# Nine waits moved or shortened in a one-core kernel: mixer, feed-forward changes, latent attention

## The reference, cut to what matters

```python
for i in range(2):
    h = h + 0.5 * swiglu(rmsnorm(h, ln_ffn1[i]), w1_gate[i], w1_up[i], w1_down[i])   # 1024 -> 2816 -> 1024
    u = rmsnorm(h, ln_mix[i])
    h = h + (mamba2_mixer(u, ...) if i == 0 else latent_attention(u, ...))
    h = h + 0.5 * swiglu(rmsnorm(h, ln_ffn2[i]), w2_gate[i], w2_up[i], w2_down[i])
    h = h + (p[i] @ w_ple_in[i]) * sigmoid(rmsnorm(h, ln_ple[i]) @ w_ple_gate[i])
    if i == 0: latent keys = rmsnorm(rmsnorm(h, ln_kv) @ w_kv_a)      # shared by all streams
```

## Time and profile before

| | |
|---|---|
| median of 3 runs | 1906.42 us (1904.54 to 1907.23) |
| the profiled execution's own time | 1900.23 us |
| its span in the profile | 1898.4 us |
| PE busy in the span | 1832.8 us, 97% |
| DVE, ACT, POOL busy | 1140.4, 825.7, 249.8 us |
| the chain that ended last | PE 83%, DVE 9%, ACT 4% |

### The profile page before, as it was taken

The page is one execution under the profiler, slowest core; times in us unless marked ns, Lnnn a source line. Parts: engine busy times, 40 slices in busy tenths (PEclk is TensorE's granted clock), DMA queues, the critical chain, the costliest instruction groups (busy, mean ns, idle before and its releaser), DMA issues.

```text
span 1898.4 us, 28238 instructions
## 1 busy us (share of the span) xinstructions
PE 1832.8 (97%) x10552; PEld 1742.0 (92%) x10552; DVE 1140.4 (60%) x1703; ACT 825.7 (43%) x1425; POOL 249.8 (13%) x298
## 2 busy tenths in 40 slices
PE   9999999999999999999999999988998999999997
PEld 8999998798887899999999999985777889999997
DVE  6554447878888655444765544455777746455444
ACT  5333325665464433333553333345665534333233
POOL 1000110422221000011400001222112130000110
PEclk9999999999999999999999999999999999999999
DMA  6444444456352544444344444441124533444441
GB/s 204 128 119 129 134 143 145 151 189 227 117 200 84 176 127 120 129 145 133 112 142 122 121 132 142 136 140 37 45 82 128 170 118 113 133 125 121 142 136 64
DMA packets 67652, 249.71 MB, mean 132 GB/s; under 512 B 8328, under 2 KB 9608, under 8 KB 66288
## 3 DMA queue, kind: packets, MB, share of 16 engines
q1 hardware_dynamic: 57584, 205.32, 35.9%
q0 software_dynamic: 9984, 43.24, 6.8%
HBM read 235.74 MB, written 12.12 MB: 131 GB/s over the span
## 4 chain that ended last, share of the span: by engine, by line
PE 83%; DVE 9%; ACT 4%; issue 2%; DMA 1%; POOL 0%; SPq 0%; DVEq 0%; ACTq 0%; POOLq 0%
PE pair L1805 23%; PE pair L1806 23%; PE pair L1807 23%; PE pair L2300 1%; PE pair L2218 1%; DVE wlo L1195 1%; PE pair L2219 1%; PE pair L2220 1%; DVE cy L1321 1%; PE pair L1812 1%; PE pair L1814 1%; PE pair L1813 1%; ACT seg L835 1%; PE pair L2002 1%; DVE S L1417 1%
## 5 line engine op out<-in xcount | busy, mean ns | idle before, releaser
L1805 PE MATMUL pair<-xh,whi 128*128 128x384 f32 x1928 | 652.9, 339 | 16.2 <-DVE xl L1205 13.4
L1806 PE MATMUL pair<-xl,whi 128*128 128x384 f32 x1928 | 647.1, 336 | 0.0
L1807 PE MATMUL pair<-xh,wlo 128*128 128x384 f32 x1928 | 646.9, 336 | 0.0
L1195 DVE TENSOR_TENSOR wlo<-raw,whi 128x1024 fp32r<-128x1024 f32 (+3 forms) x372 | 464.7, 1251 | 185.4 <-ACT whi L706 176.1
L706 ACT ACTIVATE whi<-raw 128x1024 fp32r<-128x1024 f32 (+2 forms) x369 | 378.7, 1029 | 290.8 <-PE pair L1807 276.7
L1805 PEld LDWEIGHTS pair<-xh,whi 128*128 128x128 f32 x1928 | 364.1, 189 | 26.3 <-issue 14.9
L1806 PEld LDWEIGHTS pair<-xl,whi 128*128 128x128 f32 x1928 | 364.3, 189 | 1.6 <-issue 1.0
L1807 PEld LDWEIGHTS pair<-xh,wlo 128*128 128x128 f32 x1928 | 364.1, 189 | 0.0
L1215 DVE TENSOR_TENSOR tg<-pair,rstd 128x384 f32<-128x384 f32 x88 | 49.0, 557 | 331.2 <-PE pair L1807 330.5
L1805 PE MATMUL pair<-ah,whi 128*128 128x384 f32 x704 | 237.0, 337 | 3.5 <-DVE tu L1216 3.3
L1807 PE MATMUL pair<-ah,wlo 128*128 128x384 f32 x704 | 236.6, 336 | 0.0
(11 more groups left out here) (394 smaller groups left out, 2285.1 us busy)
## 6 DMA issues: line engine op xcount, KB each, us to landing
raw<-in_stream SPq DMA_DIRECT2D x372, 512.0 KB, 3.6
S<-in_ssm POOLq DMA_DIRECT2D x4, 2048.0 KB, 9.2
out_ssm_s<-S POOLq DMA_DIRECT2D x4, 2048.0 KB, 8.1
seg<-acs_rows POOLq DMA_DIRECT2D x12, 512.0 KB, 6.1
cTb<-in_cacheT POOLq DMA_DIRECT2D x10, 512.0 KB, 4.0
kn<-rs_rows SPq DMA_DIRECT2D x16, 264.0 KB
lowC<-in_cache SPq DMA_DIRECT2D x8, 512.0 KB, 3.2
lowA<-in_cacheT POOLq DMA_DIRECT2D x6, 512.0 KB, 5.2
```

The source lines that it names most:

```text
L1195: V.tensor_tensor(wlo[:, r, 0:w], raw[:, r, 0:w], whi[:, r, 0:w].bitcast(F32), ALU.subtract).then_inc(lo_ready, 1)
L1805: M(out, whi[:, r, ws], mh_(k), start=first and k == k0, stop=False)
L1806: M(out, whi[:, r, ws], ml_(k), start=False, stop=False)
L1807: ins = M(out, wlo[:, r, ws], mh_(k), start=False, stop=last and k == k1 - 1)
```

## The change

It touches nine places. The arithmetic is the same but for two forms (the last of the y squares is added by PE; the compressed queries are scaled once, straight from PSUM). In the listing "..." marks what is left out.

1. **Mixer's order.** In table and engine programs: `in 0, in 1, in 2, out 0, in 3, out 1, in 4` in place of `in 0, in 1, out 0, in 2, out 1, in 3, in 4`.
2. **State products.** Four in a call, in four banks; two calls in a group. The first call stands between y tiles 1 and 2, the second behind `in 1` of the next group (last group: behind the first output block).
3. **Mixer's end.** Three y squares are summed on POOL, the fourth by a second matmul. POOL does `last_part`. `residual(2)` and `(3)` follow each other, weight splits move behind what PE waits for, the state adds move behind the norm's sums.
4. **Feed-forward.** `down` waits for the first last pair only, and for the second before its third product.
5. **Behind KV.** The splits of h go ahead of the token norm; PE waits for `kvr` before its third block.
6. **Compressed queries.** The 512-wide copies are gone; each token tile is finished on its own in the last block.
7. **First prompt scores** go ahead of half of the values; key weights, values and past splits are interleaved.
8. **First units.** The first maximum goes ahead of the last two absorbed parts, the second key split behind the first unit; Exp is loaded three parts earlier.
9. **Sample heads.** Two head pairs per bank in four banks; the first output block starts by the tile; the last two output blocks run side by side, so that the splits of h begin seven tiles before the end.

```diff
-order += [("in", g, 0), ("in", g, 1), ("out", g - 1, 0), ("in", g, 2), ("out", g - 1, 1), ("in", g, 3), ("in", g, 4)]
+order += [("in", g, 0), ("in", g, 1), ("in", g, 2), ("out", g - 1, 0), ("in", g, 3), ("out", g - 1, 1), ("in", g, 4)]
...
+            return bank[(6, 7, 4, 5, 4, 7, 5, 6)[i] if g == GROUPS - 1 else (6, 7, 4, 5, 4, 5, 0, 3)[i]]
...
 (POOL, last group)
+                    pool.wait_ge(y_rstd, 1)
+                    pool.wait_ge(f_evac, 8 * g)
+                    pool.tensor_tensor(facc[:, 6:8, :], facc[:, 6:8, :], bc(rstd[:, 0, :], (P, 2, TOK), 1),
+                                       ALU.mult).then_inc(h_part, 1)
+                    pool.wait_ge(h_part, 1)
+                    pool.tensor_tensor(h[:, 6:8, :], h[:, 6:8, :], facc[:, 6:8, :], ALU.add).then_inc(h_part, 1)
...
 (DVE, group g)
                     in_proj(g, 1)
+                    state_add(g - 1, 2)
                     state_add(g - 1, 3)
-                    out_proj(g - 1, 0)
                 in_proj(g, 2)
+                    out_proj(g - 1, 0)
...
 (DVE, mixer's end)
-            last_part()
-            for b in range(4):
+            for b in range(2):
                 residual(b)
+                lo_split(n + 4 + b)
                 x_lo(2, 2 * b)
                 x_lo(2, 2 * b + 1)
-                if b < 3:
-                    lo_split(n + 4 + b)
+            residual(2)
+            residual(3)
+            for k in range(4, KD):
+                x_lo(2, k)
+            lo_split(n + 6)
...
 (DVE, compressed queries)
-            for t in range(TT):
-                V.tensor_scalar(cqr[:, t, :], bank[t][:, :], rows[:, 1, t:t + 1], None, ALU.mult).then_inc(cq_ready, 1)
             dve.wait_ge(w_ld, 16 * 5)
             for t in range(TT):
                 dve.wait_ge(cq_std, t + 1)
                 step(V.reciprocal(rsc[:, t, 4:5], rsc[:, t, 2:3]))
+                step(V.tensor_tensor(rsc[:, t, 4:5], rsc[:, t, 4:5], rows[:, 1, t:t + 1], ALU.mult))
...
 (PE)
             def down(u, m):
-                pe.wait_ge(gu_evac, 2 + KF * (u + 1))
+                pe.wait_ge(gu_evac, 1 + KF * (u + 1))
                 for j in range(KD):
+                    if j == 2:
+                        pe.wait_ge(gu_evac, 2 + KF * (u + 1))
...
+                for j in range(4):
                     rows32 = slice(32 * j, 32 * j + 32)
+                    ins = M(state_bank(g, 4 * e + j)[:, :], Bm[rows32, e, :], xw[rows32, 2, :], start=True, stop=True)
...
-            M(bank[5][:, 0:TOK], ones[:, :], sqacc[:, 0, :], start=True, stop=True).then_inc(y_sum_ps, 1)
+            M(bank[5][:, 0:TOK], ones[:, :], sqacc[:, 0, :], start=True, stop=False)
+            pe.wait_ge(y_sq, 4 * GROUPS)
+            M(bank[5][:, 0:TOK], ones[:, :], zs[:, 3, :], start=False, stop=True).then_inc(y_sum_ps, 1)
...
+            pe.wait_ge(q_kept, 12)
+            p_values(0)
+            p_values(1)
+            pe.wait_ge(key_kept, 4)
+            pe.wait_ge(key_rows_ready, ITEMS)
             p_scores(0)
             p_scores(1)
+            p_values(2)
+            p_values(3)
+            pe.wait_ge(wk_lo, 2)
...
+            for k in range(KD):
+                for b in (6, 7):
+                    ins = product(bank[2 + b % 4][:, 0:TOK], (WO + b) % SLOTS, k, k + 1, *X, k == 0, k == KD - 1)
+                    if b == 6 and k == KD - 1:
+                        ins.then_inc(blk, 1)
+                if k < KD - 1:
+                    ins.then_inc(wo_ps, 1)
```

More of the change, by code:

```diff
@@ L935, in _ @@
             kx_hi(KD - 1)
-            for b in range(3):
-                hi_split(KV + b + 3)
+            hi_split(KV + 3)
+            hi_split(KV + 4)
+            act.wait_ge(blk, CRED + PG + KD)
+            for k in range(KD - 2):
+                x_hi(4, k)
+            hi_split(KV + 5)
+            for k in range(KD - 2, KD):
+                x_hi(4, k)
             def token_std(m, x):
@@ L1124, in _ @@
                 ins.then_inc(qc_hi, 1)
+                if j == 5:
+                    act.preload_act_table(ACT.Exp)
                 if j == 3:
@@ L1206, in x_lo, with gate_up @@
                                        in1=xh[:, k, :].bitcast(F32), op0=ALU.mult, op1=ALU.subtract).then_inc(xl_ready, 1)
-            def gate_up(u, m, norm_sums=None):
+            def gate_up(u, m, norm_sums=None, behind=None):
                 base, r = BASE[f"gu{u}"], rstd[:, m % 2, :]
@@ L1224, in pair @@
                         V.tensor_tensor(al[:, f, :], tu[:, j, :], ah[:, f, :].bitcast(F32), ALU.subtract).then_inc(al_ready, 1)
-                lo_split(base + 3)
                 if norm_sums is not None:
                     norm_sums()
+                lo_split(base + 3)
+                if behind is not None:
+                    behind()
                 if m != 4:
@@ L1444, in out_proj @@
                 f_add(g, b)
-            def last_part():
-                step(V.tensor_tensor(facc[:, 6:8, :], facc[:, 6:8, :], bc(rstd[:, 0, :], (P, 2, TOK), 1), ALU.mult))
-                V.tensor_tensor(h[:, 6:8, :], h[:, 6:8, :], facc[:, 6:8, :], ALU.add).then_inc(h_part, 1)
             def residual(b):
@@ L1513, in _ @@
                 y_rows(g)
-                if not last:
-                    state_add(g, 2)
             n = out_block(GROUPS - 1, 0)
@@ L1550, in _ @@
             kx_lo(KD - 1)
-            for b in range(3):
-                lo_split(KV + b + 3)
+            lo_split(KV + 3)
+            lo_split(KV + 4)
+            for k in range(KD - 2):
+                x_lo(4, k)
+            lo_split(KV + 5)
+            for k in range(KD - 2, KD):
+                x_lo(4, k)
             def token_rows(x):
@@ L1748, in _, with absorbed @@
             keys_split(0)
-            for j in range(8):
+            def absorbed(j):
                 dve.wait_ge(qc_hi, j + 1)
@@ L1755, in _ @@
                 ins.then_inc(qc_ev, 1)
+            for j in range(6):
+                absorbed(j)
             def s_max(u):
@@ L1769, in _ @@
             s_max(0)
-            keys_split(1)
+            absorbed(6)
+            absorbed(7)
             for u in range(UNITS):
@@ L1789, in _ @@
                 V.tensor_tensor(h[:, b, :], h[:, b, :], bank[2 + b % 4][:, 0:TOK], ALU.add).then_inc(h_new, 1)
-            for k in range(KD):
+            lo_split(WO + 9)
+            for k in range(6):
                 x_lo(6, k)
+            for b in (6, 7):
+                dve.wait_ge(blk, CRED + WO + b + 1)
+                V.tensor_tensor(h[:, b, :], h[:, b, :], bank[2 + b % 4][:, 0:TOK], ALU.add).then_inc(h_new, 1)
+            x_lo(6, 6)
+            x_lo(6, 7)
+            lo_split(WO + 10)
             gate_up(3, 6)
@@ L1830, in pair @@
                         pe.wait_ge(gu_evac, i * 2 + (KF * u + j + 1))
+                        if first and j and m == 4:
+                            pe.wait_ge(kvr_ready, TT)
                         for half in range(2):
@@ L2343, in _ @@
                     pe.wait_ge(h_new, 48 + b - 3)
-                product(bank[2 + b % 4][:, 0:TOK], (WO + b) % SLOTS, 0, KD, *X, True, True).then_inc(blk, 1)
+                for k in range(KD):
+                    if b == 0 and k % 2 == 0:
+                        pe.wait_ge(ol_ready, MH // 2 + k // 2 + 1)
+                    ins = product(bank[2 + b % 4][:, 0:TOK], (WO + b) % SLOTS, k, k + 1, *X, k == 0, k == KD - 1)
+                ins.then_inc(blk, 1)
+            weights(WO + 6)
+            weights(WO + 7)
+            pe.wait_ge(h_new, 48 + 4)
+            for k in range(KD):
+                for b in (6, 7):
+                    ins = product(bank[2 + b % 4][:, 0:TOK], (WO + b) % SLOTS, k, k + 1, *X, k == 0, k == KD - 1)
+                    if b == 6 and k == KD - 1:
+                        ins.then_inc(blk, 1)
+                if k < KD - 1:
+                    ins.then_inc(wo_ps, 1)
+            ins.then_inc(blk, 1)
             gate_up(3, 6)
```

205 lines of the change are left out of this document (102 added, 103 removed).

## The result

The changed kernel takes 1872.08 us (median of 4 runs, 1871.61 to 1874.61), the kernel before 1905.48 in the same comparison. The ratio is 0.9829, with a 95% interval of 0.9814 to 0.9843: 32.6 us less (30 to 35). Forecast were 1878.0 in a range of 1869 to 1889, and 28.5 us of gain. The profiled execution takes 1872.35 us, 27.9 less than the profiled one before. The medians lie 33.4 apart, since the profiled execution before, at 1900.23, was a short one of its kernel.

The account below looks back on a forecast made before the run. PE, busy 97% of the span, was taken as the bound. Gains 3.0 + 7.0 + 4.2 + 2.2 + 0.5 + 4.9 + 1.0 + 5.7 = 28.5 us off the 1906.4 median gave 1878 us, range 1869 to 1889.

Parts of the forecast that it names:

- A: Mixer's groups: four-product calls and new block order gain 3.0 us despite new waits for S; bounds −0.5 to 5.
- E: Compressed queries: gain 0.5 us, mostly hidden behind the transfer of wv; bounds 0 and 4.8.
- D: Behind KV: gate_up(2) no longer waits for xl, less 0.7 of new wait; gain 2.2 us, bounds 0 to 3.
- F: First prompt scores: waits vanish, second expansion of past keys begins at 1317.1; gain 4.9 us, bounds 2 to 6.
- G: First units: second unit's scores wait less for Pb, unit 2 comes 0.5 to 1.1 earlier; gain 1.0 us.
- B: Mixer's end: shorter DVE chain to the last xl, POOL helping, half clock shrinking; gain 7.0 us, bounds 2.5 to 10.
- the first rival: Mixer's groups and units: clock falls in the new waits, each fall costing 1.5 us; total 1883; chance 0.15.
- The third rival: Mixer's end: POOL blocks DVE, costing 5.6 in place of 1.5 us; total 1882; chance 0.08.
- C: Start of down: waits for tu vanish at three of four, 1.4 us each; gain 4.2 us, bounds 3.3 to 4.5.
- H: Heads and output: heads take 3.8 us, block begins 2.7 earlier, gate_up(3) waits go; gain 5.7 us, bounds 3 to 6.5.
- The second: State products: four not side by side, a call takes 2.3 us; some 3 us lost, total 1881; chance 0.11.
- The slower one: New waits for S, at the units and behind KV leave half-clock stretches that eat the gain; ≥ 1910; chance 0.02.

Follow-up runs that it names:

- x_pool_late: Changed kernel, with POOL summing the y squares of groups 0 to 2 only behind the second output block; 1867.77 us, ratio 0.9809.
- x_both: Changed kernel, with POOL's y square sum later and DVE's third pair of state adds before the second input block; 1863.53 us, ratio 0.9779.
- x_a_undone: Changed kernel, with output blocks back in place and state products two in a call for groups 0 to 2; 1871.61 us, ratio 0.9829.
- x_last_dve: Changed kernel, with scaling and adding of the last two tiles of h at the mixer's end moved from POOL to DVE; 1868.87 us, ratio 0.9810.
- x_w_split: Changed kernel, with the three small loads counted apart from wk and wv ahead of the compressed queries; 1871.03 us, ratio 0.9819.
- x_s_early: Changed kernel, with DVE adding the third pair of states before the second input block; 1874.61 us, ratio 0.9851.
- x_again: The changed kernel once more, without an edit; 1873.19 us, ratio 0.9835.

## Why the prediction was right, and which steps failed

**The total** was right, 1878 against 1872.1, in a range of 1869 to 1889. The sum was 28.5 us and the profiled executions lie 27.9 apart, but in this two errors meet: A with the stretch ahead of it is 7.4 short, E, D, F and G are 6 over and B is 1 over. That they cancel is luck. By medians the gain is 33.4. At most some 8 of the 27.9 us came through the clock, an estimate from the mean granted clock of the two executions: 0.990 over 1898 us and 0.994 over 1871 us leave 19 and 11 us of full clock not granted. The sum named such a gain in B (2.5) and in D alone.

**A. Products of the groups**, 3.0 forecast, −0.9 measured in their stretch. Step by step: the call was taken as 1.45 between bounds of 1.2 and 2.3 and is 1.07, below the lower bound, since 1.2 had been read up to the second matmul behind the call (364.98), past a restart. Nothing but the restart is paid for the second pair. The new wait for `S` was worked out as 2.2 and is 1.97, 2.25, 2.24. The step that failed is "the wait of 0.44 for `facc` also goes, as DVE is ahead by then". DVE was not ahead: the first output block's add now comes behind input block 2, into POOL's squares, and the wait grew to 0.98 and 1.60. x_pool_late and x_both show this. With some 1.6 us of half clock at the third place, in its stead, that is 4.2 us, about the distance from 3.0 to −0.9. The price of such a meeting stood in the earlier trace rows, and I used it for B alone. Also, one of the three waits for `S` drew a half clock (PEclk 0.85 and 0.81 in 525 to 535 us), so the first rival's mechanism came true once of three times. Its price did not: where half clock stood, the wait for `facc` behind it was gone (see x_a_undone).

**The stretch ahead of A**, 3.5 us lost, was in no part of the sum. It varies from 23.4 to 26.3 us in three profiles of before's stage order and from 23.4 to 26.9 in ten of the changed one's. The sum took the profiled execution's clock as that of every execution.

**B. Mixer's end.** 5.95 to the norm's sum and 2.09 ahead of it, 8.0 of 7.0. In that, POOL's price was 0.6 too low: 1.5 forecast, 2.14 measured. It cancels the 1.9 that the sum gave to `last_part`. The third rival was right in its mechanism (full blocking) and too high in price, as for part of POOL's 5.1 us DVE had an operation that reads PSUM and a split begun before POOL's, and neither was slowed. The new start wait of 1.61 and the norm sum's 1.40 (2 forecast) came, the wait for `xl` fell from 3.97 to 2.17, and PEclk was 1.00 from 600 to 625 in the first profile, but 0.93 in those of x_last_dve, x_w_split, x_s_early and x_a_undone.

**C** gave 3.84 up to the first matmul of each `down` and, with 0.11 each from its shorter first step (197.77 − 197.49 = 0.28 before, 0.17 after), 4.2 of 4.2. The step for the restart was right.

**D** gave 3.13 and 0.87 in the stage behind, 4.0 of 2.2. The wait of 0.7 for `lo_split(base + 3)` was 0.23, and the 2.9 was too low: the wait of 2.56 and the half clock behind it, which cost 1.7 (PEclk 0.66 from 953 to 958 before), make 4.3.

**E** gave 3.67 of 0.5. The bound by `wv` was right: the first reciprocal waits 2.46 us for its landing, 11.6 us after the issue, and the three tiles follow at 1.05. The product starts 1.3 earlier, 0.5 of it since the transfer itself took 11.6 us in place of 12.2. The other 2.4 are the half clock that stood behind it before (PEclk 0.50 from 1255 to 1260) and not in the first profile of the changed kernel. It stands again in four of the ten profiles of changed kernels: shorter in those of x_again and x_w_split (0.66 and 0.68 from 1240 to 1245), as long in those of x_last_dve and x_both (0.86 from 1225 to 1250). The part's sum had no term for it; these 2.4 us are luck of the execution.

**F** gave 5.62 of 4.9: the second expansion starts 19.8 us before where it was, the key split's wait is 0.17 (0.45 forecast) and no half clock follows (PEclk 0.66 from 1318 to 1323 before). **G** gave 1.50 of 1.0, but not by its mechanism. Of the 1.50, 0.47 is the wait ahead of the heads, which the sum had in H. The wait of 2.98 became 2.10 and 1.75, and PE's waits of the whole stretch sum to 9.8 us after as against 9.9 before. What was won is the half clock that stood behind the 2.98 (PEclk 0.66 from 1447 to 1452 before); x_again has one there again. **H** gave 5.05 of 5.7, 5.5 with that 0.47: the heads take 1507.99 − 1504.02 = 3.97 us (3.8 forecast), and all waits of its stages are gone.

**Rivals.** The second (four products not side by side) is out: 1.07. The slower one is out. The fifth, that E gains nothing, is out, by 1.3 us without the clock.

## What to carry to other kernels

Where a wait is moved or shortened, find the engine whose list it hangs on and follow that list to the next consumer: two limits in a row hide each other, and only taking both away pays in full (−1.4 and 5.4 us alone, 9.7 together). Before work is given to POOL, count what it takes from DVE's operations with two SBUF inputs in that window; here 1.90 us of help cost 2.14, and sums that nobody waits for cost PE 2.6 us of waits by where they stood. Keep apart what a profile shows of the program and what it shows of the execution: one stretch of the same work took between 23.4 and 26.9 us in thirteen profiles, so a sum of parts is best read from the ends of each part, and a gain that is half clock gone is to be looked for in a second profile before it is believed.

## What the runs showed of the hardware

- Four 32-row products of 512 columns in four row strips and four banks take 1.07 us from start to the next instruction, in all eight calls of the changed kernel; two take 1.05.
- DVE's operations with two SBUF operands (768 columns) beside a POOL operation end 0.82 us after POOL's end, twice, in place of 0.96 us after their own start; one that reads PSUM, and a split that had begun 0.21 us before POOL's, kept their 0.94 and 1.16. Beginning first did not always protect: the split at 453.13 began 0.43 us before POOL's first addition, though 0.15 behind POOL's DMA issue, and took 2.56.
- POOL's four additions cost DVE 3.4 us in 5.6. POOL lost too: its second addition, beside that split, took 1.89 us where the third and fourth took 1.24.
- The granted clock from 320 to 345 us was between 0.80 and 0.93 in the mean in thirteen profiles, in work that is the same but for its shift of some 2 us; in the first units 1.00 and 0.96 in two executions of one kernel.
